# A hybrid encoder trunk on one core: the gated-delta mixer rebuilt as a pipeline with a block solve on VectorE

## The reference, cut to what matters

```
qkv = silu(centred_depthwise_conv(z[..., :3 * W], conv_w))
q, k = l2_normalize(heads(q)), l2_normalize(heads(k)); q = q * dk ** -0.5
log_decay = -exp(A_log) * softplus(a + dt_bias);  beta = sigmoid(b)
gcum  = cumsum(log_decay) in a chunk
decay = exp(where(i >= j, gcum_i - gcum_j, -inf))
a_mat = where(i > j, (k * beta) k^T * decay, 0)
sol   = (I + a_mat)^-1 [v * beta, k * beta * exp(gcum)] = u, w
v_new = u - w state
o     = (q * exp(gcum)) state + (q k^T * decay) v_new
state = state * exp(g_last) + (k * exp(g_last - gcum))^T v_new
```

## Time and profile before

| | |
|---|---|
| median of 3 runs | 4829.43 us (4828.25 to 4837.86) |
| profiled execution | 4829.25 us, span 4827.6 us |
| mean granted TensorE clock | 0.875 |
| TensorE busy | 3675.4 us (76%) |
| VectorE busy | 2213.1 us (46%) |
| ScalarE busy | 1090.2 us (23%) |
| GpSimd busy | 261.2 us (5%) |

### The profile page before, as it was taken

One profiled execution on the slowest core, in us unless ns is written; L12 is line 12 of the kernel. 1 busy time (PEld: TensorE's weight loads), 2 busy tenths in 40 slices (PEclk: granted clock), 3 DMA queues, 4 the chain that ended last, 5 costly groups with the idle time before them and its releaser, 6 DMA issues. The chain is left out here.

```text
span 4827.6 us, 52395 instructions
## 1 busy us (share of the span) xinstructions
PE 3675.4 (76%) x17350; PEld 2377.6 (49%) x17350; DVE 2213.1 (46%) x4878; ACT 1090.2 (23%) x2308; POOL 261.2 (5%) x357
## 2 busy tenths in 40 slices
PE   8799999699999688885565499708968846539970
PEld 1245555488888688884233244304446623314430
DVE  0222330599997466663787100171145525520017
ACT  0011222244444222221111022101134411102210
POOL 0000000100000000000000200010000000020101
PEclk9899999699998799997777699859989977869995
DMA  7612222401110111114231499842122141139984
GB/s 254 204 58 59 67 60 66 154 29 38 38 38 20 51 35 35 35 36 80 103 118 64 161 362 365 282 162 94 63 81 65 60 113 69 69 134 363 366 299 161
DMA packets 383410, 592.63 MB, mean 123 GB/s; under 512 B 61042, under 2 KB 266906, under 8 KB 383022
## 3 DMA queue, kind: packets, MB, share of 16 engines
q1 hardware_dynamic: 313934, 368.18, 24.6%
q10 hardware_dynamic: 47776, 151.99, 8.1%
q0 software_dynamic: 21584, 71.00, 4.5%
HBM read 466.29 MB, written 124.81 MB: 122 GB/s over the span
## 5 line engine op out<-in xcount | busy, mean ns | idle before, releaser
L373 PE MATMUL inp__bank<-inp__hT,inp__w 128*128 128x512 f32 (+1 forms) x1536 | 559.9, 524 | 10.3 <-DMA inp__w<-in_ab_w_in_dram 8.3
L2156 PE MATMUL moe__bank<-moe__wgu,moe__xT 128*128 128x512 f32 x1024 | 456.4, 599 | 14.1 <-DMA moe__wgu<-in_moe_w_up_dram 12.5
L373 PEld LDWEIGHTS inp__bank<-inp__hT,inp__w 128*128 128x128 f32 x1536 | 290.4, 191 | 272.5 <-issue 252.1
L1789 PE MATMUL close__bank<-close__w_out,close__catT 128*128 128x512 f32 x640 | 311.7, 649 | 102.0 <-DVEq L1930 95.3
L2156 PEld LDWEIGHTS moe__bank<-moe__wgu,moe__xT 128*128 128x128 f32 x1024 | 191.2, 192 | 235.1 <-issue 221.9
L1789 PEld LDWEIGHTS close__bank<-close__w_out,close__catT 128*128 128x128 f32 x640 | 132.3, 210 | 271.3 <-issue 186.0
L2279 DVE TENSOR_TENSOR moe__hid<-moe__sg,moe__bank 128x256 f32<-128x256 f32 x64 | 27.0, 421 | 481.2 <-ACT moe__sg L2218 481.2
L2173 PE MATMUL moe__bank<-moe__wdn,moe__hidT 128*128 128x512 f32 x512 | 230.5, 593 | 2.9 <-ACT moe__hidT L2222 2.9
L2474 PE MATMUL qkv__bank<-qkv__w,qkv__hT 128*128 128x512 f32 x480 | 210.7, 596 | 2.7 <-DVE qkv__hT L2566 2.7
L410 ACT ACTIVATE inp__z<-inp__bank 128x512 f32<-128x512 f32 (+1 forms) x96 | 50.5, 526 | 654.4 <-PE inp__bank L373 654.4
L247 PE MATMUL ada__bank<-ada__w,ada__c_silu 128*2 128x512 f32 x384 | 170.6, 600 | 30.6 <-DMA ada__w<-in_ada_w_dram 29.0
(11 more groups left out here) (404 smaller groups left out, 6518.1 us busy)
## 6 DMA issues: line engine op xcount, KB each, us to landing
moe__wdn<-in_moe_w_down_dram ACTq DMA_DIRECT2D x64, 1024.0 KB, 8.6
moe__wgu<-in_moe_w_gate_dram SPq DMA_DIRECT2D x64, 1024.0 KB
moe__wgu<-in_moe_w_up_dram SPq DMA_DIRECT2D x64, 1024.0 KB
ada__w<-in_ada_w_dram SPq DMA_DIRECT2D x24, 2048.0 KB, 8.0
scratch_y_rows<-moe__y ACTq DMA_DIRECT2D x64, 512.0 KB
scratch_zt<-inp__tb SPq DMA_DIRECT2D x32, 640.0 KB, 4.9
inp__w<-in_ab_w_in_dram POOLq DMA_DIRECT2D x31, 512.0 KB, 4.6
delta__qkv<-scratch_zt SPq DMA_DIRECT2D x20, 768.0 KB, 4.7
```

The costliest lines, as they stand in the source:

```text
L373: mm = nc.tensor.matmul(zbank[j][g][:, 0:n], w[:, j, k, :], hT[:, k, t0:t0 + n], start=k == 0, stop=k == KC - 1)
L1789: mm = pe.matmul(bank[2 + c][:], catT[:, k, :], w_out[:, k, c * 512:(c + 1) * 512], start=k == 0, stop=k == KC - 1)
L2156: mm = pe.matmul(bank[2 + j][:], xT[:, j, k, :], wgu[:, j, k].rearrange("p a n -> p (a n)"), start=k == 0, stop=k == KC - 1)
```

## The change

In `input_projection`: for chunks 12 to 19 VectorE squares and sums the transposed chunk by head, GpSimd takes the power -1/2, VectorE scales the chunk in place, and only then SyncE stores it. So `zt` holds normalized queries and keys. VectorE's loop over the convolutions is written out, and so is GpSimd's over these weight loads, with the powers between them.

```
+                def head_norm(c):
+                    dve.wait_ge(t_ev, 3 * c + 6)
+                    nlink(nc.vector.tensor_tensor(sqs[:], tb[:, j], tb[:, j], ALU.mult))
+                    nlink(nc.vector.tensor_reduce(rn[:], sqs[:], AX.X, ALU.add))
+                    nc.vector.tensor_scalar(rn[:], rn[:], 1e-12, None, ALU.add).then_inc(norm_in, 1)
+                def head_scale(c):
+                    dve.wait_ge(rooted, n + 1)
+                    nc.vector.scalar_tensor_tensor(tb[:, j], ...rn...).then_inc(normed_r, 1)
+                    if CONV0 < c <= CONV0 + 8:        # behind the convolution of chunk c
+                        head_norm(c - 1)
+                        head_scale(c - 1)
+                        for c in range(first, first + 10):                       # GpSimd
+                            pool.wait_ge(z_mm, 3 * c + 3)
+                            pool.dma_start(w[:, c % 2], ...).then_inc(w_loaded[c % 2], 16)
+                            if c >= first + 2:
+                                pool.wait_ge(norm_in, n + 2)
+                                pool.tensor_tensor(rn[:], rn[:], power[:], ALU.pow).then_inc(rooted, 1)
```

```
+                for s in range(-3, NT):                                       # TensorE
+                    from_state(s)        # 16 products 128x128
+                    level5(s + 1)        # waits: placed(s + 1), masks(s + 2)
+                    g_rows(s + 3)        # 8 products with gb, 8 with the floor
+                    solved_for(s)
+                    level5_apply(s + 1)
+                    out_and_state(s)
+                    turned(s + 3, (0, 1, 2))
+                    level6(s + 1)
+                    turned(s + 3, (3, 4, 5))
+                    level6_apply(s + 1)
+                    products(s + 3)      # waits: gt_ev, inverse of s + 1 copied
+                for s in range(-3, NT):                                       # ScalarE
+                    stack(s + 2)         # waits: all four masks of s + 2
+                    place(s + 1)
+                    level5(s + 1)
+                    decays(s + 3)        # 8 exponentials 128x128
+                    solved_copy(s)       # 8 scaled 128x128 and 2 plain 128x512 copies
+                    level5_apply(s + 1)
+                    turned(s + 3, (0, 1, 2))
+                    level6(s + 1)
+                    turned(s + 3, (3, 4, 5))
+                    keys(s + 4)          # 8 scaled copies
+                    level6_apply(s + 1)
+                    values(s + 1)        # 8 scaled copies
+                for s in range(-3, NT):                                       # VectorE
+                    right_side(s)        # waits: from_state(s)
+                    masked(s + 2)
+                    block_solve(s + 2)   # state(s) behind rows 3, out(s) behind rows 5
+                for s in range(-3, NT):                                       # GpSimd
+                    gather_kv(s + 1)
+                    spread(s + 4)        # gb, the log decays along 128 columns
+                    gather_qk(s + 5)
+                    clear(s + 1)
+                    scatter_o(s)
```

Each call stands only for tiles 0 to 9 (the conditions are left out here, and the comments are added). Core of the new helpers:

```
+                def right_side(i):
+                    for d in range(2):
+                        dve.wait_ge(ks_mm, 2 * i + d + 1)
+                        for h in range(4):
+                            ins = dve.scalar_tensor_tensor(rhs[...], bank[d][...], col(nbg, i, 4 * d + h), vb[...], ALU.mult, ALU.add)
+                    for d in range(2):
+                        dve.wait_ge(qs_mm, 2 * i + d + 1)
+                        dve.tensor_tensor(qs[:, d], bank[2 + d][:], eg[...], ALU.mult)
+                def state(i):
+                        for d in range(2):
+                            dve.wait_ge(s_mm, 2 * i + d + 1)
+                            for h in range(4):
+                                ins = dve.scalar_tensor_tensor(S[:, 4 * d + h], S[...], col(eg[:, 1], ...), bank[d][...], ALU.mult, ALU.add)
+                def gather(dst, part, i, sem):
+                    pool.indirect_dma_start(out=dst, out_offset=None, in_=rows512,
+                                            in_offset=bass.IndirectOffsetOnAxis(ap=back[:, part, i:i + 1], axis=0))
```

More of the change, by code:

```diff
@@ L63 @@
 CONST_W = _at
-LEVELS = 7
 DECAY = math.exp(-0.5)
@@ L115, in constant_tables @@
     which = [0] + [1] * (TP - 2) + [2] + [0] + [1] * (TILES - TP - 2) + [2]
-    return {"const_f": c, "const_levels": levels.reshape(P, -1), "const_rope": rope,
+    tokens = np.concatenate([np.arange(last * P - 1, first * P - 1, -1) for first, last in SEQ_TILES]).reshape(TILES, P).T
+    back = np.stack([tokens * CHUNKS * P // GD_W + (RWC * P // GD_W + n) for n in range(3)] + [T + tokens], 1).astype(np.int32)
+    return {"const_f": c, "const_rope": rope, "const_back": np.ascontiguousarray(back),
             "const_tok": (np.arange(P)[:, None] + P * np.arange(TILES)[None, :]).astype(np.int32),
@@ L506, in _ @@
                 dve.wait_ge(cb_ready, RWC + 2)
[L507 to L522, removed]
@@ L553, in units @@
     return bank[:].rearrange("p (q t) -> p q t", q=4)
[L556 to L638, removed]
@@ L1373, in run_turns @@
[L1373 to L1378, removed]
-                turn(last - 1, total, last if last < TILES else None)
+        DD = ph.sb("DD", [P, 8, P])
+        kT = ph.sb("kT", [P, 4, 8, P])
+        bqT = ph.sb("bqT", [P, 4, 8, 2, P])
+        BP = ph.sb("BP", [P, 3, 8, 2, P])
+        S = ph.sb("S", [P, 8, P])
@@ new lines, in deltanet_mixer @@
+        vec, vec_s, cleared, kb_r, vb_r, grow, dd_e, tr, tr_ev, prod, prod_ev, stacked, n_read, solved, placed = (ph.sem(n) for n in (
+            "vec", "vec_solve", "cleared", "kb_ready", "vb_ready", "g_rows", "diff_exp", "turned", "turned_ev", "products", "products_ev",
+            "stacked", "lanes_read", "solved", "placed"))
+        y5_mm, y5_ev, x64_mm, x64_ev, y6_mm, y6_ev, gt_mm, gt_ev, x_clear = (ph.sem(n) for n in (
+            "y5_mm", "y5_ev", "x64_mm", "x64_ev", "y6_mm", "y6_ev", "inverse_mm", "inverse_ev", "x_cleared"))
@@ L1381, in deltanet_mixer, with mirror, col @@
+        def mirror(i):
+            first, last = SEQ_TILES[i >= TP]
+            return first + last - 1 - i
+        def col(t, i, n):
+            return t[:, 8 * i + n:8 * i + n + 1]
         with nc.Block() as block:
@@ new lines, in level5 @@
+                def level5(i):
+                    pe.wait_ge(placed, 8 * i + 8)
+                    if i > 1:
+                        pe.wait_ge(x_clear, i - 1)
+                    if have(i + 1):
+                        pe.wait_ge(prod_ev, 4 * (i + 1) + 4)
+                    for e in range(2):
+                        for h in range(4 * e, 4 * e + 4):
+                            mm = pe.matmul(bank[4 + e][:, (h % 4) * P:(h % 4 + 1) * P], BP[:, i % 3, h, 0, :], X[:, i % 2, h, :],
+                                           start=True, stop=True)
+                        mm.then_inc(y5_mm, 1)
@@ L1635, in mod_row @@
+                for s in range(-3, NT):
+                    if have(s):
+                        right_side(s)
+                    if have(s + 2):
+                        masked(s + 2)
+                        block_solve(s + 2)
+                    elif have(s):
+                        state(s)
+                        out(s)
 def mod_row(a, m, q, part):
```

754 lines of the change are left out of this document (494 added, 260 removed).

## The result

| | before | after |
|---|---|---|
| median | 4828.84 us, 4 runs (4822.19 to 4837.86) | 4634.55 us, 4 runs (4626.43 to 4640.65) |
| profiled execution, span | 4829.25, 4827.6 us | 4635.21, 4633.5 us |
| mean granted clock | 0.875 | 0.861 |
| DeltaNet stage, first load to the next stage's | 644.2 us | 443.5 us |

What follows compares the result with a forecast made beforehand. Before, a serial inverse chain through three engines bound the kernel; afterwards, program order would. Fill 93, seven steps of 43 (301) and tail 77 make 471 us against 644: 4829.25 - 173 = 4656 us, range 4575 to 4725.

Steps and rivals of the forecast that it cites:

- The pause ahead of level 5: DeltaNet step: TensorE idles some 9 us until ScalarE, queued behind right side, masks and stack, has placed the solved blocks.
- The second pause: DeltaNet step: TensorE waits 3.4 us ahead of the masked products because ScalarE scales keys before copying the inverse.
- TensorE's work: DeltaNet steady step: products and transpositions sum to 26.3 us at full clock, against 61.7 a turn before.
- VectorE and ScalarE: DeltaNet steady step: VectorE's operations sum to 25.1 us, ScalarE's copies and per-head operations to about 24.
- The clock: TensorE in the DeltaNet step: slow work behind its two waits adds 2.6 and 1.4 us.
- The step: DeltaNet stage: one steady step takes 39 us at full clock plus 4 for slow clock, 43 us.
- Fill: DeltaNet stage start: first masks at 40 us, then 20 and 33 more, so step 0 begins at 93.
- Tail: DeltaNet stage end: from step 7 nothing new is fed; the last tile and its scattered store end 77 us later.
- All the rest stays as it is: Whole program outside the DeltaNet stage and the input stage: stays unchanged.
- The input stage: Input projection: norms on eight chunks and the later weight load cost 0 us, upper bound 1 us x 8.
- The pause isn't there: DeltaNet step: ScalarE gets ahead and TensorE's queue stays full; step 29, total 4540, chance 0.12.
- The clock stays low: TensorE, level 5 to output: 14.3 us of work doubles; step 55, total 4755, chance 0.12.

Runs made afterwards that it cites:

- the filled pause: Changed kernel with 28 idle 128x128 products put into TensorE's wait ahead of level 5: 4624.6 us, ratio 0.958 to the kernel before.
- all four reorderings: Changed kernel, ScalarE placing before stacking and copying the inverse before keys, VectorE masking before right side, SyncE loading key/value rows before query/key rows: 4531.3 us.
- the next improvement: Changed kernel with ScalarE's copy of the finished inverse ahead of the scaled keys: 4623.9 us, ratio 0.958 to the kernel before.
- one tile in flight: Changed kernel's operations kept, but each engine finishes its part of a tile before taking the next: 4824.7 us, ratio 1.000 to the kernel before.
- placing first: Changed kernel with ScalarE's copies that place the solved blocks ahead of its copies of the decayed blocks: 4587.1 us, ratio 0.950 to the kernel before.
- masks first: Changed kernel with VectorE's masks ahead of its right side, ScalarE's order kept: 4581.3 us, ratio 0.949 to the kernel before.

## Why the prediction was right, and where it was off

- **What bounds it.** Right. The pause ahead of level 5 was put at 9 us and is 8.5, ended by ScalarE's placing, and the order ahead of it came almost to the tenth (masks done 6.9 us after the step's start, stack 8.7, placing 12.2, against 7.2, 9.1 and 12.6); three experiments moved it with the order of two engines' programs and nothing else. The second pause was put at 3.4 and is 2.5: a per-head operation of ScalarE, taken at 0.35 us, runs at 2.44 / 8 = 0.30, and the keys start (1802.07) before TensorE has ended level 6 and its apply (1802.49), not behind it.
- **TensorE's work**, 26.3 us. 204.17 / 279 of a step is 30.1; less the slow clock (1.7 at level 5, 1.7 at the products) 26.7. And with the pauses out the step came to 28.2.
- **VectorE and ScalarE**, 25.1 and 24. By the same row 23.2 and 21.5. Both a little high, neither on the path. VectorE waits 10.5 us in the solve, not 8.
- **The clock**, 2.6 + 1.4 = 4.0 us a step: 1.7 + 1.7 = 3.4 (by the distance to the next group of products). The sum was near; the split was wrong, since I took the second, shorter pause for half harmless. The rule of the Trainium skill (TensorE: Matmul & The Clock Gate, Why this matters for your kernels), against idle gaps, was borne out: behind the filled pause level 5 took 2.05 us in place of 3.64, and the stage 9.9 us less.
- **The step**, 43: 41.1. **Fill**, 93: 86.4, with the first masks done at 36, not 40. **Steady steps**, 301: 284.2, of which 13 by the shorter step and the rest since the last interval has no keys left to scale and took 37.4. **Tail**, 77: 72.9. Stage 471: 443.5. All four erred to one side. Of the 2 us of step, 0.6 is the clock and 1.4 the two pauses; the fill was 4 us shorter up to the first masks and 3 behind them.
- **A microsecond of step is 8.3 in all.** From after to all four reorderings the stage lost 105.3 us for 12.9 of step: 8.2.
- **What I missed in the mixer**: the key and value load behind another load in SyncE's queue. It cost nothing in the changed kernel (the load moved alone: step the same) and took back all of the steady step's gain from the next improvement. I had followed GpSimd's queue in order, and SyncE's not.
- **"All the rest stays as it is"** was wrong by 8.7 us: the router stage. It is longer in all thirteen profiles of changed kernels (472.4 to 475.6 us against 465.5 in the one profile before), that with one tile in flight among them, so it doesn't come from the flight. TensorE waits there for VectorE's queue, about 1 us more a tile. The cause was not tried and is open. With it the sum closes: 4829.25 - 200.7 + 8.7, and 1.6 from an earlier start of the stage, is 4635.7 against 4635.2. So the total came nearer than its parts: the stage saved 28 us more than forecast, and the router stage took 9 of them back, by luck.
- **The input stage**, 0: right. It kept its length, and the weight load, issued behind the power at 551.09 and 4.4 us to landing, was there 3 us ahead of its products (558.65): the cover was better than I thought.
- **The rivals.** "The pause isn't there" needed the order of the RWKV mixer, placing first; with masks first and the loads in place too, it gave 4531, where I had put 4540. "The clock stays low" is not what happened: it was at 1.00 from 1785, 4 us after the start of level 5. GpSimd, at 0.95 to 0.98 us a gather and 1.3 a scatter, was far from the bound.

## What to carry over

When work is spread over stages in flight, write down each engine's program as a queue and ask of each entry whether its input is a step older than that of the entry ahead of it: the older one goes first. Two such exchanges here were worth 91 us, nearly half as much as the whole rebuild. A pause costs twice, once by itself and once by the clock behind it. And when a gain fails to arrive, look at the loads: an edit that seems to do nothing may only be waiting for the next one.

## What was not expected of the hardware

- A pause of 2.5 us can be enough for TensorE to run part of the next 16 instructions at 1.2 GHz: ahead of the masked products of the changed kernel in every steady step (5.41 us against 3.72, granted clock 0.57 from 1805 to 1807). But it isn't always: with placing first the same pause left them at 3.72 in four of seven steps, and behind pauses of 2.49 us ahead of level 5, with masks first, level 5 took 2.05 us in four steps and 3.4 to 3.6 in three others. After 0.8 us or less it fell in none of the steps read here.
- The end of a product in the record is not the moment at which others see it: beside two pairs of additional gathers VectorE was released 2.6 us after it, though TensorE had gone on to its next products at 1775.50. The Trainium skill (Perfetto Trace Analysis, Tensor Engine Instruction (MATMUL, LD_WEIGHTS)) says that this end is an estimate; the rows above agree, but don't tell whether the products ended late or their signal came late.
